# A hybrid Hyena/attention layer: output projection by Strassen's seven products instead of eight

## The chip, the cores and the metric

One NeuronCore of one Trainium2 chip. The metric is the device time of one execution in microseconds (us), lower is better. A measurement of this kernel tells differences of some 0.2% from none.

## The reference

One layer over 512 latent tokens and 256 context tokens of width 2048. The tokens are normalised and modulated, projected to 4928 columns, and go through three groups of heads (a long convolution, attention with 8 heads, and pooling), whose outputs side by side are again 2048 wide. The part that changes is the last product and what surrounds it:

```python
out_l = mixer(u_l, keys_all, lp, rope, True)      # (1, 512, 2048)
x_l = x_l + gt * (out_l @ w_out[l])               # w_out: (2048, 2048), gt: (1, 1, 2048)
return rmsnorm(x_l, final_norm_g)                 # over the 2048 columns of each token
```

## The kernel before

All five engines run programs of their own, written out by hand, and wait for each other on semaphores; the order of work on an engine is the order in the code. DMAs are issued by SyncE (SP), a few by ScalarE.

TensorE multiplies rounded float32 numbers only, so every operand x is split in two: ScalarE writes its rounded part (`_hi`), VectorE the remainder x - hi (`_lo`), and TensorE sums three products, hi*hi, hi*lo and lo*hi. The 2048 columns of the mixed heads lie transposed in the tile UG, 16 blocks of 128 rows with 512 tokens each: 0 to 3 from the convolution, 4 to 11 from attention, 12 to 15 from pooling.

The output projection goes by four blocks b of 512 output columns and four pieces c of 512 rows of w_out, 16 pieces of 1 MB. For each piece n = 4b + c:

- SyncE loads it to one of three places `wo_raw` once the piece three before it is done (`load_out`, L547).
- ScalarE rounds it into one of two tiles `wo_hi` once the piece two before it is done (`wo_high`, L1031); VectorE writes the remainder over the raw weights (`wo_low`, L1687).
- TensorE multiplies it by four groups of 128 tokens, each 4 x 3 products into its own PSUM bank (`out_part`, L2370), 48 products in all. The stationary operand is the left side (128 x 128), the moving one the weights (512 columns).

The left side is split once, by block of UG (`mixed`, L1021 and L1675). At the end of a block b VectorE multiplies each token group's bank by the gate (L1695) and adds x (L1697, tile `y`), ScalarE takes the squares (L1038), and GpSimd multiplies by the gain (L657). For the last block the gate is multiplied into the weights instead (`gate_into`, L1683), and the four token groups end one after another: sum, squares, root, reciprocal, scaling (L1697, L1038, L1197, L1922, L1203, L1926, L1927), then the stores.

The first piece's four groups are spread between the last steps of attention, as fillers.

## Time and profile before

| | |
|---|---|
| median of 3 runs | 921.84 us (921.84 to 921.89) |
| span of the profiled execution | 920.1 us, 1.7 below that median |
| own time of the profiled execution | not listed apart from the span |
| TensorE matmuls | 906.8 us busy, 99% of the span |
| VectorE, ScalarE, GpSimd busy | 70%, 43%, 13% |
| output projection after attention | 749.9 to 913.1 us |
| after the last product | 7.0 us |

A busy share is a mean over stages with different limits. The durations of matmuls overlap: the distance from one start to the next counts, not the 0.39 us of one. "Idle before" is how long an engine stood still ahead of an instruction, with what released it.

### The profile page before, as it was taken

Reading aid. Unit: us, or ns where it says so; the run is one execution under the profiler, and the core shown is the slowest. Engines: PE = TensorE matmul, PEld = TensorE weight load, DVE = VectorE, ACT = ScalarE, POOL = GpSimd, SP = SyncE. Lnnn points to the kernel's source line nnn. Section 1 sums busy time; section 2 is a strip of 40 time slices with the busy share of each in tenths; the row PEclk is TensorE's granted clock in tenths of the full one; section 3 lists DMA queues with packets and bytes.
Section 4 is the critical chain, followed back from the end, with each engine's and each line's share of the span. In section 5 each row is a group of like instructions: output and inputs, shape, how many; then the busy total and the mean of one; then the engine's idle time right before and its main releaser. Section 6 shows DMA issues by size and latency. Waiting matters only on the chain.

```text
span 920.1 us, 12214 instructions
## 1 busy us (share of the span) xinstructions
PE 906.8 (99%) x4850; PEld 756.7 (82%) x4850; DVE 641.1 (70%) x839; ACT 396.0 (43%) x615; POOL 115.6 (13%) x107
## 2 busy tenths in 40 slices
PE   9999999999999999999999999999999999999996
PEld 6777788888888888888888888889999888888885
DVE  5555898799987899867974674877777961424463
ACT  4655566535435344333233434554544551322124
POOL 1222200300003000001007731000010000202020
PEclk9999999999999999999999999999999999999999
DMA  9999923223322212287872352201010244233214
GB/s 361 416 420 422 413 101 104 92 80 97 109 82 91 69 69 92 70 323 285 298 275 93 92 172 70 69 30 40 1 58 1 92 188 179 92 101 114 105 46 182
DMA packets 29860, 137.93 MB, mean 150 GB/s; under 512 B 3531, under 2 KB 3915, under 8 KB 22892
## 3 DMA queue, kind: packets, MB, share of 16 engines
q1 hardware_dynamic: 29328, 136.50, 40.0%
q8 instruction: 38, 0.62, 0.3%
q10 hardware_dynamic: 476, 0.66, 0.2%
q14 instruction: 18, 0.15, 0.1%
HBM read 131.25 MB, written 4.19 MB: 147 GB/s over the span
## 4 chain that ended last, share of the span: by engine, by line
PE 89%; DMA 5%; DVE 2%; ACT 2%; issue 1%; SPq 0%; POOL 0%; ACTq 0%; DVEq 0%
PE pp L2058 40%; PE pp L2370 19%; PE pp L2088 17%; DMA ada_raw<-in_w_ada_dram 5%; PE pp L1973 3%; PE pp L1949 2%; PE pp L2334 2%; PE pp L1979 1%; PE pp L2326 1%; PE pp L2325 1%; DVE softmax_stats L1644 1%; ACT U L996 1%; DMA ada_raw<-in_w_scale_dram 1%; DVE pt_lo L1659 0%; PE pp L2157 0%
## 5 line engine op out<-in xcount | busy, mean ns | idle before, releaser
L2058 PE MATMUL pp<-h_hi,w_hi 128*128 128x512 f32 x544 | 213.0, 392 | 0.0
L2058 PE MATMUL pp<-h_hi,w_lo 128*128 128x512 f32 x544 | 211.8, 389 | 0.0
L2058 PE MATMUL pp<-h_lo,w_hi 128*128 128x512 f32 x544 | 211.8, 389 | 0.0
L1359 DVE TENSOR_TENSOR w_lo<-w_raw,w_hi 128x1024 fp32r<-128x1024 f32 x68 | 89.3, 1313 | 68.6 <-ACT w_hi L787 67.9
L787 ACT ACTIVATE w_hi<-w_raw 128x1024 fp32r<-128x1024 f32 x68 | 71.8, 1056 | 129.4 <-PE pp L2058 129.4
L2058 PEld LDWEIGHTS pp<-h_hi,w_lo 128*128 128x128 f32 x544 | 102.1, 188 | 21.5
L2058 PEld LDWEIGHTS pp<-h_hi,w_hi 128*128 128x128 f32 x544 | 102.2, 188 | 21.1 <-DVE w_lo L1359 0.3
L2058 PEld LDWEIGHTS pp<-h_lo,w_hi 128*128 128x128 f32 x544 | 102.2, 188 | 20.5
L2370 PE MATMUL pp<-wo_hi,m_hi 128*128 128x512 f32 x256 | 99.7, 390 | 0.0
L2370 PE MATMUL pp<-wo_hi,m_lo 128*128 128x512 f32 x256 | 99.6, 389 | 0.0
L2370 PE MATMUL pp<-wo_lo,m_hi 128*128 128x512 f32 x256 | 99.6, 389 | 0.0
L1687 DVE TENSOR_TENSOR wo_lo<-wo_raw,wo_hi 128x2048 fp32r<-128x2048 f32 x16 | 36.7, 2291 | 82.4 <-ACT wo_hi L1031 82.4
L1031 ACT ACTIVATE wo_hi<-wo_raw 128x2048 fp32r<-128x2048 f32 x16 | 30.6, 1914 | 86.9 <-PE pp L2370 86.9
L2370 PEld LDWEIGHTS pp<-wo_hi,m_lo 128*128 128x128 f32 x256 | 48.1, 188 | 10.1
L2370 PEld LDWEIGHTS pp<-wo_hi,m_hi 128*128 128x128 f32 x256 | 48.0, 188 | 10.0
L2370 PEld LDWEIGHTS pp<-wo_lo,m_hi 128*128 128x128 f32 x256 | 48.1, 188 | 9.8
L1004 ACT ACTIVATE pt_hi<-pp 128x768 fp32r<-128x768 f32 x32 | 26.0, 812 | 50.3 <-PE pp L2334 50.0
L1659 DVE TENSOR_TENSOR pt_lo<-pp,pt_hi 128x768 fp32r<-128x768 f32 x32 | 30.4, 952 | 19.1 <-ACT pt_hi L1004 19.1
L996 ACT ACTIVATE U<-pp,softmax_stats 128x768 f32<-128x768 f32 x32 | 28.9, 904 | 23.8 <-DVE softmax_stats L1646 23.6
L657 POOL TENSOR_TENSOR y<-y,gain 128x512 f32<-128x512 f32 x12 | 15.5, 1297 | 180.0 <-ACT out_tmp L1038 179.7
L1371 DVE SCALAR_TENSOR_TENSOR gate_acc<-w_gate_raw,silu_c,gate_acc 128x2048 f32<-128x2048 f32 x15 | 35.2, 2346 | 1.5 <-DMA w_gate_raw<-in_w_gate_dram 1.5
L1949 PE MATMUL pp<-ada_raw,silu_spread 128*32 128x256 f32 (+1 forms) x544 | 32.3, 378 | 3.9 <-DMA ada_raw<-in_w_ada_dram 2.7
(348 smaller groups left out, 1794.0 us busy)
## 6 DMA issues: line engine op xcount, KB each, us to landing
w_raw<-in_wb_dram SPq DMA_DIRECT2D x68, 512.0 KB, 3.7
ada_raw<-in_w_ada_dram SPq DMA_DIRECT2D x15, 2048.0 KB, 13.4
w_gate_raw<-in_w_gate_dram SPq DMA_DIRECT2D x16, 1024.0 KB, 6.4
wo_raw<-in_w_out_dram SPq DMA_DIRECT2D x16, 1024.0 KB, 4.7
y<-in_x_dram SPq DMA_DIRECT2D x4, 1024.0 KB, 8.5
wa_raw<-in_wa_dram SPq DMA_DIRECT2D x14, 288.0 KB, 8.0
UG<-in_xT_dram SPq DMA_DIRECT2D x7, 512.0 KB, 8.8
wh_raw<-in_w_heads_dram SPq DMA_DIRECT2D x4, 768.0 KB, 4.6
```

The lines of the kernel that those rows point to most:

```text
L787: eng.activation(lane(wb_hi, n % 2), lane(wb_raw, n % KW), ACT.Copy).then_inc(wb_hi_done, 1)
L996: eng.activation(prob(n % 3).rearrange("p (a b) -> p a b", a=2), psum[:, 2 * (n % 2):2 * (n % 2) + 2, 0:384], ACT.Exp, bias=st[:, 4 * s + ...
L1031: eng.activation(wo_high_[n % 2][:], wo_raw[n % 3][:], ACT.Copy).then_inc(wo_hi, 1)
L1359: eng.tensor_tensor(lane(wb_lo, n % KW), lane(wb_raw, n % KW), lane(wb_hi, n % 2), ALU.subtract).then_inc(wb_lo_done, 1)
L1371: eng.scalar_tensor_tensor(out=gate_acc[:], in0=w, scalar=c, in1=gate_acc[:], op0=ALU.mult, op1=ALU.add).then_inc(row_sums, 1)
L1659: eng.tensor_tensor(lo, psum[:, 4:6, :].rearrange("p a b -> p (a b)")[:, 0:LK].rearrange("p (k q) -> p k q", k=6), hi, ALU.subtract).then_ ...
L1687: eng.tensor_tensor(wo_low_[n % 3][:], wo_raw[n % 3][:], wo_high_[n % 2][:], ALU.subtract).then_inc(wo_lo, 1)
L1949: mm = eng.matmul(ps[7][32 * strip:32 * strip + 32, 256 - n:256], spread[:, 32 * kk:32 * kk + 32], ada[b % 3][:, kk * n:(kk + 1) * n], sta ...
L1973: mm = eng.matmul(ps[i][:], w, x, start=first and n == 0, stop=last and n == len(xs) - 1)
L2058: mm = eng.matmul(ps[i][:], w, x, start=(kk == 0 and m == 0), stop=(kk == KT - 1 and m == 2))
L2088: mm = eng.matmul(dst, w, x, start=first and m == 0, stop=last and m == 2)
L2370: mm = eng.matmul(psum[:, 4 * (b % 2) + tok, :], a, v[:, w:w + L], start=(kk == 0 and m == 0), stop=(kk == 15 and m == 2))
```

## The change

Tokens, rows and columns are each halved: the left side A into A11, A12, A21, A22 (tokens x rows of w_out; the row halves are pieces 0, 3 and 1, 2 of each column block, so the blocks of UG 0 to 3, 12 to 15 and 4 to 11), w_out into B11 to B22. Seven products of halves, numbered 1 to 7, take the place of eight; each is two column blocks b by two pieces c, 28 chunks in the order of `CHUNKS`, of 24 products each (two token groups). Their left sides are single halves or differences, their right sides single halves (products 1, 2, 3) or sums of halves of w_out.

- The sums of weights are made by DMA: SyncE loads one piece to a place `wo_sum` (`load_sum`), and GpSimd issues DMAs that add another piece of w_out to it in place (`add_weights`); the sums of 7, 6 and 4 are made one from the other.
- The left sides of 7, 6, 5 and 3 are made by GpSimd (`side`), in halves of 1024 columns, over UG itself but for that of 7. All left sides are split when their product comes (`side_high`, `side_low`), not once.
- Products 2, 4, 5 and 3 go on accumulating in the banks that hold 1, 7, 6 and 6 + 5 (`BANKS`); what other blocks need of products 1 and 7 is copied out by ScalarE (`hold`), 6 without 1 by VectorE (`without_first`), and GpSimd multiplies the copies by the gate and subtracts them from x ahead of time (`subtract_ahead`).
- The gate is multiplied on VectorE for all blocks (`block_out`). The tokens 256 to 511 end first (`LAST_TOKENS`), and the last two groups in one chunk, 27.
- x is loaded in two halves, y_left and y_right, the second after chunk 17, since it lies where the side of 6 was.

```diff
+CHUNKS = [(1, 0, 0), (1, 1, 0), (1, 0, 1), (1, 1, 1)] + [(u, b, c) for u, b in (
+    (7, 0), (6, 0), (4, 0), (2, 0), (2, 1), (7, 1), (6, 1), (4, 1), (5, 0), (5, 1), (3, 0), (3, 1)) for c in range(2)]
...
+SIDES = (1, 7, 6, 4, 2, 5, 3)
+PLACE = {1: 0, 7: 1, 6: 2, 4: 3, 2: 0, 5: 0, 3: 3}
...
+def summed(n):
+    u, b, c = CHUNKS[n]
+    if u == 5:
+        return (c + 2, 1, 1) if b == 0 else (c, 3, 7)
+    return c, b + 1, 3 * b + {7: 1, 6: 2, 4: 3}[u]
...
+            eng.wait_ge(wo_mm, chunk_of(7, 1, 1) + 1)
+            for c in range(2):
+                load_sum(chunk_of(5, 0, c))
+            eng.wait_ge(wo_mm, chunk_of(6, 1, 1) + 1)
+            for i in range(4):
+                eng.dma_start(y_right[:, 2 * i * L:2 * (i + 1) * L], t["x"][i * P:(i + 1) * P, 1024:D]).then_inc(y_in[1], 16)
+            for c in range(2):
+                eng.wait_ge(wo_lo, chunk_of(4, 1, c) + 1)
+                load_sum(chunk_of(5, 1, c))
+            for n in range(24, 28):
                 load_out(n)
...
+            def side(u, c):
+                if u == 7:
+                    made(eng.tensor_tensor(side_raw(7, c), mixed_part(0, 0, c), mixed_part(0, 1, c), ALU.subtract))
...
+            def add_weights(n):
+                u, b, c = CHUNKS[n]
+                i, loads, added = summed(n)
+                if u in (6, 4):
+                    eng.wait_ge(sum_added[i], 16 * added - 16)
+                    eng.wait_ge(wo_lo, chunk_of(7 if u == 6 else 6, b, c) + 1)
+                else:
+                    eng.wait_ge(sum_in[i], SUM_FROM[i] + 16 * loads)
+                eng.dma_start(wo_sum[i][:], w_out(u == 4, u in (7, 5), b, c), accum_op=ALU.add).then_inc(sum_added[i], 16)
...
+            def subtract_ahead(b):
+                g = gate_rows_[:, (2 + b) * L:(3 + b) * L]
+                eng.wait_ge(held6, 2 * b + 2)
+                for x in (product1[b], product7[b]):
+                    link(eng.tensor_tensor(x[0][:], x[0][:], g, ALU.mult))
+                    link(eng.tensor_tensor(x[1][:], x[1][:], g, ALU.mult))
+                for i in range(2):
+                    y = y_block(2 + i, 2 + b)
+                    link(eng.tensor_tensor(y, y, product7[b][i][:], ALU.subtract))
+                    eng.tensor_tensor(y, y, product1[b][i][:], ALU.subtract).then_inc(side_made, 1)
...
...
+            eng.wait_ge(y_in[1], 32 + 64)
+            eng.wait_ge(held, 8)
+            add_weights(chunk_of(5, 1, 0))
+            subtract_ahead(0)
+            add_weights(chunk_of(5, 1, 1))
+            subtract_ahead(1)
+            gains((2, 1), (3, 1), (2, 2), (3, 2), (2, 3), (3, 3), (0, 2), (1, 2))
...
+            side_high(1, 1)
             wo_high(2)
-            for k in range(8, 16):
-                mixed(k)
-            for n in range(3, 16):
+            wo_high(3)
+            side_high(7, 0)
+            hold(1, 0)
+            wo_high(4)
...
+                if n == 16:
+                    hold(7, 1)
+                    side_high(5, 1)
+                if n == 20:
+                    side_high(3, 0)
+                if n == 21:
+                    row_squares(2, 1)
+                    row_squares(3, 1)
...
+                if n == 25:
+                    for tok in range(2, 4):
+                        row_squares(tok, 3)
+                    for i in range(2):
+                        last_root(i)
+                        last_scale(i)
...
+            def block_out(tok, b):
+                half = b % 2
+                u = (3 if tok < 2 else 5) if b >= 2 else (2 if tok < 2 else 4)
+                n = chunk_of(u, half, 1)
+                eng.wait_ge(wo_mm, n + 1 + (n == 27 and tok == 1))
+                bank, g, y = ps[BANKS[u][half] + tok % 2][:], gate_rows_[:, b * L:(b + 1) * L], y_block(tok, b)
+                dst = bank
+                if u == 4:
+                    eng.wait_ge(held6, 2 * half + 2)
+                    link(eng.tensor_tensor(bank, bank, part6[tok % 2][:], ALU.subtract))
+                if b >= 2:
+                    eng.wait_ge(side_made, 8 + 4 * half + (tok - 1 if tok >= 2 else tok + 3))
+                if u == 5:
+                    dst = part6[tok % 2][:]
+                link(eng.tensor_tensor(dst, bank, g, ALU.mult))
+                eng.tensor_tensor(y, dst, y, ALU.add).then_inc(res_done, 1)
...
-            def gate_into(n):
-                eng.wait_ge(wo_in[n % 3], 16 * (n // 3) + 16)
-                w = wo_raw[n % 3].rearrange("p (k c) -> p k c", k=4)
-                g = gate_rows_[:, 3 * L:4 * L]
-                g = bass.AP(tensor=g.tensor, offset=g.offset, ap=[list(g.ap[0]), [0, 4], list(g.ap[1])])
-                eng.tensor_tensor(w, w, g, ALU.mult).then_inc(wo_gated, 1)
...
+            def out_part(n, tok):
+                u, b, c = CHUNKS[n]
                 eng.wait_ge(wo_lo, n + 1)
-                hi, lo = wo_high_[n % 2], wo_low_[n % 3]
+                eng.wait_ge(mix_lo, 2 * SIDES.index(u) + c + 1)
+                hi, lo, x_hi, x_lo = wo_high_[n % 2], wo_low_[n % 3], side_hi[PLACE[u]], side_lo[PLACE[u]]
                 for k in range(4):
-                    kk = 4 * c + k
...
```

**GpSimd, the last third of the output projection.** Before, the last rows of its order are the split of the pooling weights and then the gains, with no DMA:

```order
L644 TENSOR_TENSOR pool_lo0_163<-U,pool_hi0_159 128x512 [waits pool_step_p]
L647 CAST w_pool_hi_167<-w_pool_122 128x512 [waits wh_lo_done]
L648 TENSOR_TENSOR w_pool_lo_168<-w_pool_122,w_pool_hi_167 128x512 [waits pool_step_p]
L657 TENSOR_TENSOR y_152<-y_152,gain_151 128x512 [waits sq_done_o,x_rows_and_gain_in]
L657 TENSOR_TENSOR y_152<-y_152,gain_151 128x512 [waits sq_done_o] x11
```

Now accumulating DMAs (L770) stand in its order. The last two are those of chunk 22 (wo_sum0) and chunk 23 (wo_sum1); between them stands the first `subtract_ahead` (L783 to L791):

```order
L770 DMA wo_sum0_142<-in_w_out_dram 128x2048 [waits wb_in0,product_held,x_in1]
L783 TENSOR_TENSOR product1_00_149<-product1_00_149,gate_rows_146 128x512 [waits part6_held]
L784 TENSOR_TENSOR product1_01_150<-product1_01_150,gate_rows_146 128x512 [waits pool_step_p]
L783 TENSOR_TENSOR product7_00_153<-product7_00_153,gate_rows_146 128x512 [waits pool_step_p]
L784 TENSOR_TENSOR product7_01_154<-product7_01_154,gate_rows_146 128x512 [waits pool_step_p]
L787 TENSOR_TENSOR y_right_148<-y_right_148,product7_00_153 128x512 [waits pool_step_p]
L788 TENSOR_TENSOR y_right_148<-y_right_148,product1_00_149 128x512 [waits pool_step_p]
L787 TENSOR_TENSOR y_right_148<-y_right_148,product7_01_154 128x512
L788 TENSOR_TENSOR y_right_148<-y_right_148,product1_01_150 128x512 [waits pool_step_p]
L791 TENSOR_TENSOR y_right_148<-y_right_148,product1_00_149 128x512
L791 TENSOR_TENSOR y_right_148<-y_right_148,product1_01_150 128x512
L770 DMA wo_sum1_143<-in_w_out_dram 128x2048 [waits wb_in1]
```

The DMA for a chunk of weights now has ten GpSimd operations of other work in front of it.

**ScalarE, the splits of the weights near the end.** Before, four squares stand between the roundings of pieces 13 and 14:

```order
L1031 ACTIVATE wo_hi1_149<-wo_raw1_143 128x2048 [waits wo_gated,wo_bank_mm,wo_in1]
L1038 ACTIVATE out_tmp_153,row_sums_154<-y_152 128x512 [waits sq_done_o,y_done_o] x4
L1031 ACTIVATE wo_hi0_148<-wo_raw2_144 128x2048 [waits wo_gated,wo_mm,wo_in2]
L1031 ACTIVATE wo_hi1_149<-wo_raw0_142 128x2048 [waits wo_gated,wo_mm,wo_in0]
L1038 ACTIVATE out_tmp_153,row_sums_154<-y_152 128x512 [waits sq_done_o,y_done_o]
```

Now, from the rounding of chunk 19 to the rounded half side ahead of chunk 22:

```order
L1214 ACTIVATE wo_hi1_141<-wo_sum1_143 128x2048 [waits wo_mm,weight_sum1_added]
L1214 ACTIVATE wo_hi0_140<-wo_sum2_144 128x2048 [waits wo_mm,weight_sum2_added]
L1200 ACTIVATE side_hi3_128<-UG 128x1024 [waits wo_mm,side_made]
L1214 ACTIVATE wo_hi1_141<-wo_sum3_145 128x2048 [waits wo_mm,weight_sum3_added]
L1226 ACTIVATE out_tmp_159,row_sums_160<-y_left_147 128x512 [waits sq_done_o,y_done_o] x2
L1200 ACTIVATE side_hi3_128<-UG 128x1024 [waits wo_mm,side_made]
L1214 ACTIVATE wo_hi0_140<-wo_sum0_142 128x2048 [waits wo_mm,weight_sum0_added]
```

The weights' rounding comes twice as often, and half sides and squares that wait for VectorE stand ahead of the next one. The scalings of the token groups (L1197, L1203) stood behind the last rounding, that of piece 15:

```order
L1031 ACTIVATE wo_hi0_148<-wo_raw2_144 128x2048 [waits wo_gated,wo_mm,wo_in2]
L1031 ACTIVATE wo_hi1_149<-wo_raw0_142 128x2048 [waits wo_gated,wo_mm,wo_in0]
L1038 ACTIVATE out_tmp_153,row_sums_154<-y_152 128x512 [waits sq_done_o,y_done_o]
L1197 ACT_TABLE_LOAD [waits row_sum]
L1197 ACTIVATE row_scale_155<-row_sums_154,row_scale_155 128x1 [waits sq_done_o]
L1203 ACTIVATE y_152<-y_152,row_scale_155 128x512 [waits gained,row_scale_done]
L1203 ACTIVATE y_152<-y_152,row_scale_155 128x512
```

Now the scalings of two groups (L1232, L1240) stand between the roundings of chunks 25 (wo_raw1) and 26 (wo_raw2):

```order
L1226 ACTIVATE out_tmp_159,row_sums_160<-y_right_148 128x512 [waits sq_done_o,y_done_o] x2
L1214 ACTIVATE wo_hi0_140<-wo_raw0_134 128x2048 [waits wo_mm,ada_in0]
L1214 ACTIVATE wo_hi1_141<-wo_raw1_135 128x2048 [waits wo_mm,ada_in1]
L1226 ACTIVATE out_tmp_159,row_sums_160<-y_right_148 128x512 [waits sq_done_o,y_done_o] x2
L1232 ACT_TABLE_LOAD [waits row_sum]
L1232 ACTIVATE row_scale_161<-row_sums_160,row_scale_161 128x1 [waits sq_done_o]
L1240 ACTIVATE y_left_147<-y_left_147,row_scale_161 128x512 [waits gained,row_scale_done]
L1240 ACTIVATE y_left_147<-y_left_147,row_scale_161 128x512
L1232 ACTIVATE row_scale_161<-row_sums_160,row_scale_161 128x1 [waits row_sum,sq_done_o]
L1240 ACTIVATE y_left_147<-y_left_147,row_scale_161 128x512 [waits gained,row_scale_done]
L1240 ACTIVATE y_left_147<-y_left_147,row_scale_161 128x512
L1214 ACTIVATE wo_hi0_140<-wo_raw2_136 128x2048 [waits wo_mm,ada_in2]
```

What was the very end of the order before is now, for two of the four token groups, ahead of two roundings.

## Rows read from the trace of the kernel before

**Rows 1.** The page: busy time and share; clock in 40 slices.
```profile
PE 906.8 (99%) x4850; PEld 756.7 (82%) x4850; DVE 641.1 (70%) x839; ACT 396.0 (43%) x615; POOL 115.6 (13%) x107
...
PEclk9999999999999999999999999999999999999999
```

**Rows 2.** The chain that ended last, in order of time: start, length, work.
```profile
749.87 163.21 PE pp L2370 x720
```

**Rows 3.** Windows: length; busy of PE, PEld, DVE, ACT, POOL; clock; DMA share; GB/s.
```profile
750.00:913.10 163.10, 163.07 (x720) 134.69 (x718) 69.26 (x72) 45.61 (x61) 15.53 (x12) 1.00 0.34 126
913.10:920.10 7.00, 0.00 (x0) 0.00 (x0) 2.00 (x4) 2.35 (x5) 0.00 (x0) 0.69 0.57 217
```

**Rows 4.** The tile wo_raw (ns min/median/max), then one piece on two engines.
```profile
L547 SPq DMA_DIRECT2D wo_raw<-in_w_out_dram x16: 328/328/334, 685.2 to 880.5; - x16
L1683 DVE TENSOR_TENSOR wo_raw<-wo_raw,gate_rows x4: 2282/2292/2293, 852.6 to 886.7; 128x2048 f32<-128x2048 f32 x4
...
760.84 1.92 ACT L1031 ACTIVATE wo_hi<-wo_raw 128x2048 fp32r<-128x2048 f32 x1 [7.09 <-PE pp L2370]
762.79 2.29 DVE L1687 TENSOR_TENSOR wo_lo<-wo_raw,wo_hi 128x2048 fp32r<-128x2048 f32 x1 [4.78 <-ACT wo_hi L1031]
```

**Rows 5.** Timeline, idle time between the last heads (idle before, releaser).
```profile
738.98 0.81 ACT L1004 ACTIVATE pt_hi<-pp 128x768 fp32r<-128x768 f32 x1 [4.58 <-PE pp L2334]
739.67 0.75 DVE L1670 SCALAR_TENSOR_TENSOR UG<-pp,first_in,UG 128x512 f32<-128x512 f32 x1 [3.33 <-PE pp L2088]
```

**Rows 6.** Copies of ScalarE: one PSUM bank (timeline), 1024 columns (page).
```profile
715.55 0.60 ACT L976 ACTIVATE v_hi<-pp 128x512 fp32r<-128x512 f32 x1
...
L787 ACT ACTIVATE w_hi<-w_raw 128x1024 fp32r<-128x1024 f32 x68 | 71.8, 1056 | 129.4 <-PE pp L2058 129.4
```

**Rows 7.** Timeline of VectorE: gate and sum of a token's block.
```profile
786.76 0.69 DVE L1695 TENSOR_TENSOR pp<-pp,gate_rows 128x512 f32<-128x512 f32 x1
787.49 0.69 DVE L1697 TENSOR_TENSOR y<-pp,y 128x512 f32<-128x512 f32 x1
788.10 0.69 DVE L1695 TENSOR_TENSOR pp<-pp,gate_rows 128x512 f32<-128x512 f32 x1
```

**Rows 8.** Timeline of the end: last token, and ScalarE's table load before.
```profile
900.97 1.28 ACT L1197 ACT_TABLE_LOAD   x1
902.27 0.29 ACT L1197 ACTIVATE row_scale<-row_sums,row_scale 128x1 f32<-128x1 f32 x1
...
913.10 0.69 DVE L1697 TENSOR_TENSOR y<-pp,y 128x512 f32<-128x512 f32 x1 [2.28 <-PE pp L2370]
915.11 0.48 DVE L1926 TENSOR_SCALAR y<-y,row_scale 128x512 f32<-128x512 f32 x1
915.51 0.74 DVE L1927 SCALAR_TENSOR_TENSOR y<-y,row_scale,gain 128x512 f32<-128x512 f32 x1
...
915.11 1.33 ACT L1203 ACTIVATE y<-y,row_scale 128x512 f32<-128x512 f32 x2 [0.23 <-DVE row_scale L1922]
```

**Rows 9.** Window while x is loaded; median time to landing (page).
```profile
755.00:765.00 10.00, 10.00 (x46) 8.29 (x45) 5.22 (x7) 1.92 (x1) 0.00 (x0) 1.00 1.01 419
...
wo_raw<-in_w_out_dram SPq DMA_DIRECT2D x16, 1024.0 KB, 4.7
```

**Rows 10.** The tile y, GpSimd's multiply: ns min/median/max.
```profile
L657 POOL TENSOR_TENSOR y<-y,gain x12: 1292/1296/1302, 789.1 to 882.7; 128x512 f32<-128x512 f32 x12
```

**Rows 11.** VectorE's remainder of 1024 columns, then both engines from 546 us.
```profile
L1359 DVE TENSOR_TENSOR w_lo<-w_raw,w_hi x68: 1207/1226/2879, 123.1 to 546.6; 128x1024 fp32r<-128x1024 f32 x68
...
546.26 1.30 POOL L644 TENSOR_TENSOR pool_lo<-U,pool_hi 128x512 fp32r<-128x512 f32 x1
547.50 1.61 POOL L643 CAST pool_hi<-U 128x512 fp32r<-128x512 f32 x1
549.20 2.68 POOL L644 TENSOR_TENSOR pool_lo<-U,pool_hi 128x512 fp32r<-128x512 f32 x1
...
546.63 2.01 DVE L1359 TENSOR_TENSOR w_lo<-w_raw,w_hi 128x1024 fp32r<-128x1024 f32 x1 [1.95 <-ACT w_hi L787]
```

507 lines of the change are left out of this document (346 added, 161 removed).

## The prediction

> **What bounds the kernel now.** I read the page first, then the chain of waits, then the stretch of the output projection by itself. The page shows TensorE busy 99% of the span at full clock in every slice [rows 1]; the chain of waits says that nothing else decides: its longest piece is 720 products of the output projection in 163.21 us without a gap, 0.2267 us each [rows 2]. In that stretch VectorE is busy 42% of the time, ScalarE 28%, GpSimd 10%, and the DMA engines 34% [rows 3]. So fewer products shorten the kernel one for one, as long as the other engines keep each piece of weights ready. That is what I check.
>
> **How much time a piece leaves.** ScalarE starts the rounded part of a piece when the piece two before it is done; VectorE's remainder starts 1.95 us later and takes 2.29 [rows 4]: 4.24 us, with the semaphores 4.3. Before, a piece kept TensorE for 48 x 0.2267 = 10.88 us. Now it has half the rows of the left side, 24 products, 5.44 us, and the same 4.3 us of splitting: the slack falls from 6.6 us to 1.1. Whatever ScalarE or VectorE does ahead of a split beyond 1.1 us is a stall of TensorE.
>
> **The change, term by term** (T is the end of a chunk, numbers as in CHUNKS; S is the start).
>
> Removed: 8 products of 96 become 7, 768 - 672 = 96 products: 96 x 0.2267 = **-21.8**. The fillers between the last heads stay 48 products; ScalarE and VectorE have 4.58 and 3.33 us of idle time there [rows 5], which takes the second split that moves forward; 0. Also gone are four multiplies of weights by the gate on VectorE, 2.29 each [rows 4], which hid beside TensorE; 0.
>
> Waits that the written order makes, with every sum in time: **+9.7**.
> Chunk 4 (T the end of chunk 2): ScalarE takes product 1 out of the banks first (two copies of 0.6 [rows 6]), rounds the weights (1.9), then the second half of side 7 (1.06, from the 1024-column row [rows 6]); VectorE's order has both halves of that side (1.2) ahead of the weights' remainder (2.2). T + 1.2 + 1.9 + 1.1 + 1.2 + 2.3 = T + 7.7 where 5.4 is wanted: +2.3.
> Chunk 17: two copies and a half side (2.2) stand ahead of its rounding, 2.2 + 4.3 = 6.5: +1.1.
> Chunk 22 (T the end of chunk 19): VectorE's block (2,1) is three linked operations, 0.73 + 0.73 + 0.61 = 2.07 [rows 7], then half a side 1.2 (VectorE's 1024 columns [rows 11]), remainder 21 (2.2) to T + 5.5, block (3,1) to 7.5; ScalarE squares it (0.8), rounds a half side (1.0) to 9.4, and only then rounds piece 22, ready at 9.4 + 4.2 = 13.6 where 10.9 is wanted: +2.7.
> Chunk 26 (T the end of chunk 23): blocks (2,3), (3,3) and remainder 25 end at T + 4.9, the mean 0.3, table load and root 1.6, then the reciprocal and two scalings, 1.5 [rows 8], T + 8.3; the second token's chain another 1.9; then 4.2 for the piece: 14.4 against 10.9, +3.6.
>
> Tail: the last token came 5.44 us after the one before; now 2.72. VectorE is held by the token before for 0.73 (its gate, no longer folded into the weights) + 3.15 (from its sum to the end of its scalings [rows 8]) = 3.9 us, 1.2 beyond the last product, then a gate of its own, 0.73: **+1.9**.
>
> The accumulating DMAs: 16 of 1 MB, issued by GpSimd; the trace has none. From below, each is a plain load: 2.5 us of the engines at 419 GB/s, 4.7 us from issue to landing [rows 9]. From above, it loads, reads the sum back and writes: three passes, 7.5 us of engines, 9.7 to landing. I take two passes, one read more than the load (5.0 and 7.2), the middle. For the issue on GpSimd I take 0.8 us, between SyncE's 0.33 [rows 4] and GpSimd's own 1.3 for 512 columns. The Trainium skill's page Collectives: The Full Stack, section "The bandwidth ceiling", says that a reducing copy reads two sources on one ring and moves at half the rate of a plain one; no run here shows it yet, and by it the sum would be the two-pass one.
> *Chains.* In 7, 6, 4 each sum is made from the one before, so a step is 0.8 + 7.2 + 4.2 = 12.2 us against two chunks, 10.9: +1.3, twice, less the slack of 1.1, on two halves: **+3**. By one pass nothing.
> *Traffic.* From S8 to S12 (21.8 us) there are two sums, three loads, the gain (1 MB) and the accumulates of 9, 14, 15; from S16 to S20 the accumulates 18 to 21, two sums and 2 MB of x. By two passes both are about 12.6 MB, 30 us at 419 GB/s: +8 each, **+16**. By one pass about 9 MB: within 1 us of the time.
> *Chunk 23.* Its accumulate stands in GpSimd's order behind the first subtract_ahead, which needs y_right, which is loaded only after chunk 17 (T). x and one sum, 3.1 MB, 7.5 + 2.6 us: T + 10; accumulate 22, 0.8; ten GpSimd operations of 1.3, most linked (0.09): 13.8, T + 24.7; then 0.8 + 7.2 + 4.2 = T + 36.9, where 27.2 + 2.7 (chunk 22's wait) is due: **+7**. By one pass +4.5. Part of the wait of 16 to 20 falls inside this time and is not paid twice: **-8**.
>
> GpSimd beside VectorE. GpSimd's multiply is 1.30 us in every one of 12 rows, each taken when VectorE reads PSUM and one tile [rows 10]. But a remainder of VectorE (two inputs in SBUF) that began 0.37 us into a GpSimd operation took 2.01 us in place of 1.23, and one took 2.88; two GpSimd operations beside it and the next took 1.61 and 2.68, the first of them a copy [rows 11]. One waits for the other's whole operation. New work of GpSimd: 8 sums of sides at about 2.5 (1024 columns, twice 512), 20 subtractions and multiplies, 14 gains, some 66 us; VectorE's splits with two SBUF inputs: 73 us. So three remainders (6.6) and a half side (1.2) fall into the first subtract_ahead: +7.8 at 23; two into the second and the gains that chunk 26's scalings wait for: +4.4; a side's sum at chunk 3: +1. **+13**. By no exclusion 0. The Trainium skill's page SBUF — State Buffer, "Who interferes with whom", states that rule for a VectorE instruction with two SBUF inputs beside a GpSimd one that reads SBUF; the rows agree.
>
> Sum: -21.8 + 9.7 + 1.9 + 3 + 16 + 7 - 8 + 13 = +20.8. The profiled execution's span is 920.1 us, and the runs' median, 921.84, lies 1.7 us above it; what lies outside the span is not touched. 921.84 + 20.8 = 942.6, **942**.
>
> **Rivals.**
> One pass (an accumulate costs what a load does): -21.8 + 9.7 + 1.9 + 0 + 1 + 4.5 + 13 = +8.3, **930**. For it: the engines are busy only 34% now. Chance 0.22.
> Faster: the sums are never late. If they are there when ScalarE asks, at 6 to 9, 14 to 23, only order and tail are left: -21.8 + 9.7 + 1.9 = -10.2, **912**. It needs accumulates that land within 6 us and a subtract_ahead that is through 7 us sooner than I work out; it decides as soon as all lateness beyond the order's own is below 8.4 us. Against it: the 13.8 us of GpSimd work ahead of accumulate 23 come from twelve rows that agree. Chance 0.22.
> Three passes: each traffic stretch grows to 16.8 MB, 40 us, +18 in place of +8, and each chain step by 2.5: about +28, **970**. Chance 0.12.
> The forecast itself 0.42; and 0.02 for a result that is no change by accident. The products surely fall to 672, so "no effect of the change" is no rival. The clock stays out of the sum: it was 1.00 under products and 0.69 in the 7 us after the last one [rows 3], so a stall of 8 us may leave the next products slower, at most a chunk's 5.4 us more each; that is inside the upper bound.
>
> **How the numbers follow.** The two-pass case alone gives 932 to 954. The range takes in one pass and most of the faster case, and stops short of the whole of the three-pass one: 913 to 966, with 1 in 10 outside on each side. What a measurement of this kernel can tell from no change is 0.2%, 1.8 us. Faster is the rival of that name, 0.22; of the one-pass case a little lies at 920 to 924, same 0.04; the rest, 0.74, is slower.
>
> **What would show it.** Products: 672, 0.227 us each where they run. Idle time of TensorE in front of chunks 4, 17, 22 and 26 of 2.3, 1.1, 2.7 and 3.6 us, released by VectorE's remainder: the order. Idle in front of 6 to 9 and 10 to 12, 18, 19, with ScalarE waiting for the DMA of a weight sum: passes and traffic; the time to landing (4.7, 7.2 or 9.7) tells which. Chunk 23 as the longest single wait, 7 us or more, behind the first subtractions. VectorE's remainders of 2.3 us that read 2.5 to 3.6 beside GpSimd. The prediction is wrong if accumulates land as loads do, if GpSimd's subtractions are through in under 10 us, or if an accumulate's issue holds GpSimd for several us each, which would be late everywhere.

## The result: 970.6 us, 5.3% slower, where 942 was forecast

The changed kernel takes 970.58 us (median of 4 runs, 968.97 to 971.44), the kernel before 921.87 beside it: ratio 1.0526, 95% interval 1.0511 to 1.0541. The sign was forecast, the size was not: +48.7 us against +20.8, outside the range of 913 to 966. One of the eleven executions of e9_short_fill below, the profiled one, took 1272 us at a mean granted clock of 0.66 and is left out of that kernel's figures.

The page of the changed kernel (profiled execution: span 968.6 us) answers to [rows 1]: busy time of the engines, TensorE and its clock in 40 slices, and the queue of the accumulating DMAs.

```profile
PE 902.9 (93%) x4754; PEld 746.6 (77%) x4754; DVE 683.6 (71%) x857; ACT 426.7 (44%) x633; POOL 191.6 (20%) x153
...
PE   9999999999999999999999999999999896968475
...
PEclk9999999999999999999999999999999898998888
...
q0 software_dynamic: 2304, 16.78, 9.0%
```

TensorE has 96 products fewer (4850 to 4754), but holes in nearly every slice after the 31st, and in six of these nine slices its mean granted clock is below 0.9 of full speed (digit 8). Queue q0 moves the 16 accumulated pieces of 1 MB: 9.0% of 968.6 us, 87.2 us of all 16 engines, 5.45 each.

The chain that ended last (start, length, work), pieces of it between 742 and 931 us. A DMA of wo_sum is a plain load (869.90) or an accumulate (the others shown); L2671 are the products of the output projection.

```profile
742.48 15.18 DMA wo_raw<-in_w_out_dram
...
761.97 7.89 PE pp L2671 x24
...
775.65 7.96 DMA wo_sum<-in_w_out_dram
...
788.42 8.03 DMA wo_sum<-in_w_out_dram
...
801.11 13.15 DMA wo_raw<-in_w_out_dram
...
818.58 8.50 PE pp L2671 x24
...
839.40 8.13 DMA wo_sum<-in_w_out_dram
...
852.34 13.28 DMA wo_sum<-in_w_out_dram
...
869.90 18.09 DMA wo_sum<-in_w_out_dram
...
888.56 0.86 POOL wo_sum L770
...
909.30 9.40 DMA wo_sum<-in_w_out_dram
918.73 1.92 ACT wo_hi L1214
920.67 2.30 DVE wo_lo L1921
...
923.02 7.60 PE pp L2671 x24
```

In [rows 2] this stretch was one piece of 720 products. Now the chain goes from DMA to DMA and touches TensorE only between them. An accumulate that meets nothing else takes 8.0 us from its issue to ScalarE's rounding (775.65, 788.42, 839.40); the forecast had 0.8 + 7.2. In the stretches in which the DMA engines are full the same 1 MB takes 13 to 18 us in this chain, plain or accumulating. From 888.56 to 909.30 stands the first subtract_ahead, 20 us.

Two windows, with the columns of [rows 3]: chunks 5 and 6 with the end of 4 and the wait ahead of 7, then chunk 18:

```profile
770.00:788.00 18.00, 16.55 (x73) 12.96 (x71) 10.41 (x7) 11.47 (x11) 1.72 (x2) 1.00 0.91 172
...
870.00:878.30 8.30, 8.30 (x24) 6.33 (x24) 1.07 (x2) 0.72 (x1) 0.00 (x0) 0.65 1.03 252
```

In the first the DMA engines are busy 0.91 of the time, where the whole stretch had 0.34 before. In the second, after 6.3 us without products, the mean granted clock was 0.65: the products began at the lower level (1.2 GHz, 0.43 us apart) and ended at the upper (2.4 GHz, 0.227). That chunk took 8.25 us in place of 5.44.

The table adds up the places from TensorE's timeline: idle time ahead of the chunks plus what their 24 products took beyond 5.44 us, in us. (Idle time runs here from 0.227 us after the start of the last product; the figure in the profile's rows is 0.16 us smaller where there is a wait.) The forecast's +13 for GpSimd beside VectorE lies in it as 1 at chunk 3, 7.8 at 23 and 4.4 at 26, which makes +21.0 of its rounded +20.8. The last column is e8_small_short, an experiment below in which both sums cost next to nothing.

| place | forecast | changed kernel | e8_small_short |
|---|---|---|---|
| last heads | 0 | 1.8 | 1.5 |
| chunks 3, 4 | 3.3 | 7.1 | 2.3 |
| 6 to 9 | 3 | 3.9 | 0.2 |
| 10 to 12 | 8 | 11.7 | 2.4 |
| 16, 17 | 1.1 | 1.8 | 1.1 |
| 18, 19 | 8 | 14.7 | 1.5 |
| 20 to 22 | 2.7 | 5.1 | 5.3 |
| 23 | 14.8 | 14.5 | 0 |
| overlap | -8 | - | - |
| 24 to 27 | 8.0 | 7.4 | 5.8 |
| others | 0 | 0.3 | 0.2 |
| tail | 1.9 | 2.0 | 2.0 |
| products removed | -21.8 | -21.8 | -21.8 |
| sum | +21.0 | +48.5 | +0.5 |

The spans differ by 48.5 and 0.3 us, so nothing large is missing from the table. Of the 66.5 us in the third column from chunks 3, 4 to "others", 13.5 are slow products in chunks 3, 11, 18, 19, 23 and 26. What each row is worth when it is taken away is another question, and the experiments answer it differently than the table suggests.

### The profile page after: what moved, and what is told of

Its sections match the earlier page's. It is cut to its first block, busy times and chain, and to the rows that moved or that the text cites. A ratio compares the mean times of both kernels' runs of the same rounds, so it can differ in the third digit from the quotient of the medians.

```text
span 968.6 us, 12203 instructions
## 1 busy us (share of the span) xinstructions
PE 902.9 (93%) x4754; PEld 746.6 (77%) x4754; DVE 683.6 (71%) x857; ACT 426.7 (44%) x633; POOL 191.6 (20%) x153
## 4 chain that ended last, share of the span: by engine, by line
PE 72%; DMA 13%; DVE 6%; ACT 4%; POOL 2%; issue 2%; SPq 0%; ACTq 0%; POOLq 0%; DVEq 0%
PE pp L2361 38%; PE pp L2391 15%; DMA wo_sum<-in_w_out_dram 7%; PE pp L2671 5%; PE pp L2276 4%; DMA ada_raw<-in_w_ada_dram 3%; DMA wo_raw<-in_w_out_dram 3%; DVE wo_lo L1921 2%; PE pp L2252 2%; ACT wo_hi L1214 2%; PE pp L2637 2%; PE pp L2282 1%; PE pp L2629 1%; PE pp L2628 1%; DVE softmax_stats L1882 1%
## 5 line engine op out<-in xcount | busy, mean ns | idle before, releaser
L2671 PE MATMUL pp<-wo_hi,side_hi 128*128 128x512 f32 x224 | 94.9, 424 | 48.9 <-DVE wo_lo L1921 33.0
L2671 PEld LDWEIGHTS pp<-wo_hi,side_hi 128*128 128x128 f32 x224 | 45.1, 202 | 65.3 <-DVE wo_lo L1921 37.4
L2671 PE MATMUL pp<-wo_lo,side_hi 128*128 128x512 f32 x224 | 92.1, 411 | 0.0
L2671 PE MATMUL pp<-wo_hi,side_lo 128*128 128x512 f32 x224 | 92.0, 411 | 0.0
L1921 DVE TENSOR_TENSOR wo_lo<-wo_sum,wo_hi 128x2048 fp32r<-128x2048 f32 x16 | 38.1, 2384 | 52.7 <-ACT wo_hi L1214 52.7
L1214 ACT ACTIVATE wo_hi<-wo_sum 128x2048 fp32r<-128x2048 f32 x16 | 30.5, 1912 | 56.9 <-DMA wo_sum<-in_w_out_dram 50.8
L2671 PEld LDWEIGHTS pp<-wo_hi,side_lo 128*128 128x128 f32 x224 | 45.1, 201 | 10.3
L2671 PEld LDWEIGHTS pp<-wo_lo,side_hi 128*128 128x128 f32 x224 | 45.3, 202 | 9.3
L1921 DVE TENSOR_TENSOR wo_lo<-wo_raw,wo_hi 128x2048 fp32r<-128x2048 f32 x12 | 30.1, 2507 | 24.1 <-ACT wo_hi L1214 24.1
L1166 ACT ACTIVATE U<-pp,softmax_stats 128x768 f32<-128x768 f32 x32 | 28.9, 903 | 23.8 <-DVE softmax_stats L1884 23.7
L704 POOL CAST sum_hi<-U 128x768 fp32r<-128x768 f32 (+1 forms) x2 | 2.5, 1234 | 185.4 <-DVE U L1770 119.9
```

The costliest lines, as they stand in the source:

```text
L1166: eng.activation(prob(n % 3).rearrange("p (a b) -> p a b", a=2), psum[:, 2 * (n % 2):2 * (n % 2) + 2, 0:384], ACT.Exp, bias=st[:, 4 * s + ...
L1214: eng.activation(wo_high_[n % 2][:], src[:], ACT.Copy).then_inc(wo_hi, 1)
L1921: eng.tensor_tensor(wo_low_[n % 3][:], src[:], wo_high_[n % 2][:], ALU.subtract).then_inc(wo_lo, 1)
L2671: mm = eng.matmul(ps[BANKS[u][b] + tok][:], a, v[:, w:w + L], start=u in (1, 7, 6) and c == 0 and k == 0 and m == 0, stop=c == 1 and k == ...
```

## The experiments

All ratios are to the kernel before, with 95% intervals. The kernels of e3, e6, e7, e10, e11 and e12 compute everything; the others leave out part of the sums or add filler products, so only their times count. Code lines are excerpts.

### e1_plain: plain loads for the accumulates

```diff
-eng.dma_start(wo_sum[i][:], w_out(u == 4, u in (7, 5), b, c), accum_op=ALU.add).then_inc(sum_added[i], 16)
+eng.dma_start(wo_sum[i][:], w_out(u == 4, u in (7, 5), b, c)).then_inc(sum_added[i], 16)
```

> The 16 accumulating DMAs become plain loads of the same 1 MB from GpSimd's queue, so that the sum of the two pieces is left out: the output is not the reference's. Theory (an accumulate costs the DMA engines two passes): undisturbed, issue to ScalarE's rounding took 8.0 us for pieces 6, 7, 16, 17 and should fall to about 5.5; the idle time of TensorE ahead of chunks 7 to 9 (3.3 us) goes, ahead of 11 and 12 (8.6) and of 18 and 19 (10.2) falls to 1 or 2 each, ahead of 3 (4.9) to 2, ahead of 23 (12.6) to about 8.6, and with the long stalls goes most of the time that slow products take after them (13.5 to about 5): 968.6 - 26 - 8.5, about 934 us. Rival (the pass is cheap; the order of the queues and GpSimd's issues make the lateness): landing stays near 8 us and the time above 960.

946.8 us, 1.0265 (1.0248 to 1.0283): 23.8 less than the changed kernel, between theory and rival. From its page, the queue:

```profile
q0 software_dynamic: 2304, 16.78, 4.8%
```

4.8% of its span of 946.0 us is 45.4 us, 2.84 for each 1 MB, where the accumulate took 5.45. So an accumulate costs the engines 1.9 times a load. The forecast took two passes, 5.0. By the Trainium skill, page Collectives: The Full Stack, section "The bandwidth ceiling", the reducing step of a collective moves at half the rate of a copy; 5.45 against 2.84 agrees. Where nothing else was on the engines, the plain loads landed 5.1 us after their issue, in place of 8.0. The waits ahead of 7 to 9 went, that of 18 fell to 3.5 and that of 19 to nothing, that of 23 to 5.1. The time did not reach 934: slow products fell only from 13.5 to 11.9 us, where the theory had 5, chunk 11 still waited 3.9 us and the wait of 26 rose to 5.4.

### e2_small: accumulates of 64 KB

```diff
-eng.dma_start(wo_sum[i][:], w_out(u == 4, u in (7, 5), b, c), accum_op=ALU.add).then_inc(sum_added[i], 16)
+eng.dma_start(wo_sum[i][:, 0:128], w_out(u == 4, u in (7, 5), b, c)[:, 0:128], accum_op=ALU.add).then_inc(sum_added[i], 16)
```

> Each of the 16 accumulating DMAs covers 128 of 2048 columns (64 KB in place of 1 MB), so that most of the sum is left out: the output is not the reference's. With plain loads in their place the kernel took 946.8 us, 22 to 24 less. Theory (most of the lateness is bytes on the DMA engines): without these 16 MB the stalls ahead of chunks 3, 11 and 18 (2.9, 3.9 and 3.5 us with plain loads) fall to about 1 each, that of chunk 23 (5.1) stays, since GpSimd's 20 us of subtractions ahead of its accumulate stay: about 938. Rival (what matters is that another DMA stands in each chain, whatever its size): 944 or more.

937.8 us, 1.0174 (1.0157 to 1.0191). The theory held in its number: with the issues and waits all in place, it is the bytes. Nearly all of them together are worth 32.8 us: 23.8 for the second pass, 9.0 for the first. The waits ahead of 3, 11 and 18 fell to 0, 0.4 and 1.2 us. Not foreseen was that the wait ahead of 26 rose from 3.7 to 7.8 us: the first scalings, which stand ahead of remainder 26 on VectorE, waited 4.1 us for GpSimd's gains (L776).

### e3_ahead23: accumulate 23 ahead of the subtractions

```diff
-            subtract_ahead(0)
             add_weights(chunk_of(5, 1, 1))
+            subtract_ahead(0)
             subtract_ahead(1)
```

> The accumulate of piece 23 is issued ahead of the first subtract_ahead on GpSimd instead of behind it; nothing is left out. Theory (chunk 23 is late because its accumulate stands behind 20.2 us of GpSimd work): it is issued at about 890 us, lands by 899, is wanted at 910: the 12.6 us idle ahead of chunk 23 fall to 1 or less, its 24 products run in 5.4 us, not 7.4: 13 to 14 us less, about 955. Rival (its DMA would be late anyway, behind the loads of x and of the two last sums): the wait stays above 8 us and the time above 963.

969.0 us, 1.0511 (1.0496 to 1.0527): nothing gained beyond the spread of the runs. The theory was right on the wait and wrong on the time, the rival right on the time and wrong on the wait. TensorE's timeline shows the first product of chunks 23, 25 and 26 (start, length; idle before it and its releaser at the end):

```profile
912.22 0.50 PE L2671 MATMUL pp<-wo_hi,side_hi 128*128 128x512 f32 x1 [0.54 <-DVE wo_lo L1921]
...
930.12 0.79 PE L2671 MATMUL pp<-wo_hi,side_hi 128*128 128x512 f32 x1 [6.69 <-DVE wo_lo L1921]
...
944.80 0.77 PE L2671 MATMUL pp<-wo_hi,side_hi 128*128 128x512 f32 x1 [6.33 <-issue]
```

The 12.4 us ahead of 23 are 0.5, as the theory said. But 6.7 us now stand ahead of 25 (1.6 before) and 6.3 ahead of 26 (3.7), and three chunks run slow. VectorE's blocks of the right half wait for the subtractions, and its remainders stand behind the blocks:

```profile
922.19 0.69 DVE L1946 TENSOR_TENSOR part<-pp,gate_rows 128x512 f32<-128x512 f32 x1 [5.36 <-POOL y_right L788]
```

So the place of that accumulate alone was not the bound. GpSimd's two subtract_ahead, 38 us of work together, stand behind it, and whoever needs them first shows the wait; e4_short_sub tests that.

### e4_short_sub: the same, and the subtractions on 8 columns

```diff
-g = gate_rows_[:, (2 + b) * L:(3 + b) * L]
+g = gate_rows_[:, (2 + b) * L:(2 + b) * L + 8]
...
-link(eng.tensor_tensor(x[0][:], x[0][:], g, ALU.mult))
+link(eng.tensor_tensor(x[0][:, 0:8], x[0][:, 0:8], g, ALU.mult))
```

> As e3_ahead23, and each of the 20 GpSimd operations of subtract_ahead works on 8 of 512 columns: most of the subtraction of products 1 and 7 is left out, the output is not the reference's. In e3_ahead23 the 12.6 us ahead of chunk 23 went, and 6.9 and 6.5 us came ahead of chunks 25 and 26 in their place, and the time stayed at 969. Theory (the 40 us of GpSimd's two subtract_ahead are the chain there, whichever chunk waits for them, and GpSimd's operations lengthen VectorE's remainders): the waits ahead of 25 and 26 fall to the order's own, 1.6 and 3.7, remainder 21 takes 2.3 us in place of 3.4, chunks 22, 25 and 26 run fewer slow products: 13 to 16 us less, about 954. Rival (other work fills the place once more, the accumulates or VectorE's blocks): above 963.

953.9 us, 1.0338 (1.0320 to 1.0356), as the theory said: against e3_ahead23, which has the same order, GpSimd's 20 operations are worth 15.1 us; with the order it is 16.7 against the changed kernel. The waits ahead of 25 and 26 became 0 and 3.9 us. Its timeline also shows most clearly that GpSimd and VectorE exclude each other (the lock, from here on), GpSimd first, then VectorE:

```profile
892.09 2.13 POOL L784 TENSOR_TENSOR product<-product,gate_rows 128x8 f32<-128x8 f32 x1
894.30 0.20 POOL L783 TENSOR_TENSOR product<-product,gate_rows 128x8 f32<-128x8 f32 x1
...
891.87 2.29 DVE L1921 TENSOR_TENSOR wo_lo<-wo_sum,wo_hi 128x2048 fp32r<-128x2048 f32 x1
```

An operation of 8 columns, 0.20 us by itself, took 2.13 and ended with VectorE's remainder.

### e5_fill: products in the stalls, to hold the clock

```diff
+FILL = {3: 20, 11: 28, 18: 28, 19: 15, 23: 52, 26: 15}
...
+for m in range(count):
+    eng.matmul(ps[BANKS[u][b]][:], x[:, (m % 8) * P:(m % 8 + 1) * P], x[:, 0:L], start=False, stop=False, skip_group_check=True)
 eng.wait_ge(wo_lo, n + 1)
```

> Filler products on TensorE ahead of the waits of chunks 3, 11, 18, 19, 23 and 26 (20, 28, 28, 15, 52, 15 of 0.227 us, each total shorter than the idle time there); they add to a bank of the chunk, so the output is not the reference's. No wait is moved. Theory (after a stall of 3.5 us or more the granted clock is at its lower level, and the products run 0.427 us apart in place of 0.227, whatever else goes on): these six chunks run in 5.4 to 5.6 us in place of 7.2 to 8.3, 13.5 us less in all, about 955. Rival (those products are slow because weights are read beside full DMA engines, which is so at 11, 18 and 19): the lengths stay and the time stays at 966 to 969.

969.7 us, 1.0520 (1.0503 to 1.0537): nothing gained. The window of chunk 18, to be read beside the one of the changed kernel above:

```profile
872.50:878.00 5.50, 5.50 (x26) 4.55 (x25) 0.91 (x2) 0.00 (x0) 0.00 (x0) 1.00 1.02 250
```

The clock is 1.00 beside equally full DMA engines (1.02), so the rival's reason, contention, is out: five of the six chunks ran in 5.44 to 5.60 us, only 19 in 7.2 (its fillers ended 3.0 us before its wait did), 11.1 us less in the six. Yet the time stayed. Chunk 6 waited 2.6 us where it had waited for nothing, 12 waited 4.1 where it had 1.7, and these and 21 now ran slow, 6.1 us more together; the other 5 us came back as idle time. A chunk that ends sooner only waits longer for the next piece, as long as the pieces come from a chain of DMAs and GpSimd.

### e6_late_left: the left half of x behind piece 3

```diff
 eng.wait_ge(pv_mm, 8)
+eng.wait_ge(wo_hi, 4)
 for i in range(4):
     eng.dma_start(y_left...
```

> The load of the left half of x (2 MB, 4 DMAs) waits until the rounding of piece 3 has begun; nothing is left out. Theory (piece 3 lands late, at 757.7 us, because its 1 MB shares full engines with two accumulates and with this x): chunk 3's idle time falls from 4.7 to about 2 us, its slow products (7.7 us long) to about 6, and chunk 4 shows about 1 us of the order's own wait: 3 us less, 965 to 966. Rival (the accumulates of 4 and 5 alone fill the engines): no change, 968 to 969.

971.8 us, 1.0534 (1.0508 to 1.0560): nothing gained, as the rival said. Chunk 3 waited 3.4 us in place of 4.7, but it waited 3.2 us in the profiled executions of e4_short_sub and e7_order26 too, where nothing ahead of it was changed, so this difference can't be put down to the edit. At chunk 11 there were 7.3 us of idle time in place of 6.5.

### e7_order26: piece 26 ahead of the roots

```diff
+                    wo_high(26)
                     for i in range(2):
                         last_root(i)
                         last_scale(i)
```

(and the remainder on VectorE alike.)

> The rounding and the remainder of piece 26 are moved ahead of the roots and scalings of the first two tokens on ScalarE and VectorE; nothing is left out. Theory (the 3.7 us idle ahead of chunk 26 are this order's, and only the tail lies behind them, so that nothing can take their place): the wait falls below 1 us, the products of 26 run in 5.5 us in place of 7.2: 5 us less, 964 to 965. Rival (GpSimd's gains or the load of piece 26 hold it): 968 or more.

965.7 us, 1.0475 (1.0458 to 1.0493): 4.8 us gained, as the theory said. In the profiled execution chunk 26 lost its wait and its slow products, 5.5 us, and 1.8 us of wait came back ahead of chunk 27. (The spans differ by 2 us more; that lies ahead of chunk 26, where the two kernels are the same.) Behind the last chunk only the tail is left, +2.0 us in both, and it took nothing of the gain back.

### e8_small_short: both sums next to free

The edits of e2_small and e4_short_sub together.

> The small accumulates of e2_small and the short subtractions and the order of e4_short_sub together; both sums are mostly left out, the output is not the reference's. Theory (removed products -21.8, the written order's waits +9.7, the tail +1.9, and everything else was the two sums): 912, with some slow products after the one wait of 3.6 us 914, so faster than before. Rival (the loads that remain are late by themselves at half the time for each piece): 922 or more.

923.1 us, 1.0017 (1.0006 to 1.0028): the rival's number. The two edits nearly add up: 970.6 - 923.1 = 47.5 us, singly 32.8 and 16.7. And what is left is no gain: the 21.8 us of removed products are spent entirely. The timeline's first products of chunks 22 and 26, and a window over the second:

```profile
871.22 0.47 PE L2671 MATMUL pp<-wo_hi,side_hi 128*128 128x512 f32 x1 [2.91 <-issue]
...
898.80 0.47 PE L2671 MATMUL pp<-wo_hi,side_hi 128*128 128x512 f32 x1 [3.92 <-issue]
```

```profile
899.00:906.00 7.00, 7.00 (x25) 5.54 (x25) 5.67 (x9) 1.45 (x4) 4.52 (x2) 0.76 0.01 2
```

The waits of the written order were there (1.9 us at 4, 0.3 at 17, 3.1 at 22, 4.1 at 26, against 2.3, 1.1, 2.7 and 3.6), but also 1.4 at 12, 1.3 at 18 and 0.6 and 0.5 at 10 and 16, which the forecast had not listed, and two slow chunks of 1.7 us each. The rival's reason, late loads, fits only 10 and 18, where ScalarE's rounding waited for a DMA: 1.9 us. Ahead of 12 it stood behind a square that waited for VectorE's block, so again the written order, and ahead of 16 the remainder took 3.7 us in place of 2.3 beside GpSimd's gains.

### e9_short_fill: the same, with fillers ahead of 22 and 26

```diff
+FILL = {22: 10, 26: 14}
```

> e8_small_short with filler products on TensorE ahead of the waits of chunks 22 and 26 (10 and 14 of 0.227 us, each total shorter than the idle time there, 3.1 and 4.1 us); most of both sums is left out and the fillers add to a bank: the output is not the reference's. In e8_small_short these two chunks ran 7.18 us each in place of 5.44 at the lower clock. Theory (where the chain that ends last runs over TensorE's products, slow ones cost their whole length, though in e5_fill, where it ran over DMAs and GpSimd, they cost nothing): both run in 5.5 us, 3.4 less than the 923.1, about 919.7. Rival (VectorE and ScalarE bind there too, and idle time takes their place): 922.5 or more.

920.8 us, 0.9992 (0.9983 to 1.0001): 2.3 us less than e8_small_short, two thirds of the 3.4. No trace shows where the rest went. Where TensorE's products are the chain, as here, the lower clock does cost time.

### e10_dma_order: wanted first, issued first

```diff
 load_out(2)
-load_sum(5)
 load_out(3)
+load_sum(5)
...
+eng.wait_ge(wo_hi, chunk_of(2, 0, 1) + 1)
 for c in range(2):
     add_weights(chunk_of(7, 1, c))
...
 add_weights(chunk_of(4, 1, 0))
-add_weights(chunk_of(5, 0, 0))
 add_weights(chunk_of(4, 1, 1))
+add_weights(chunk_of(5, 0, 0))
```

(and on SyncE the loads in that order, the gain and both halves of x behind them.)

> Only the order of the DMAs is changed, nothing is left out: what is wanted first is issued first. Piece 3 ahead of the sum of 5, the left half of x behind piece 3; pieces 10 and 11 ahead of the sums and accumulates of 14 and 15, the gain behind pieces 12 and 13; the sum of 21 behind the landing of accumulate 18, accumulate 19 ahead of 20, the right half of x last. Theory (the stalls are bytes in the wrong order, the stretches as a whole have room): ahead of 3 and 11 the idle time falls from 4.9 and 6.7 us to 1 or 2, of 18 and 19 from 10.2 to about 6, with slow products gone 15 us less in all, about 954. Rival (the bytes of the accumulates fill the engines in any order, or chunk 23's chain over GpSimd takes the gain up): 964 or more.

961.1 us, 1.0426 (1.0410 to 1.0441): 9.4 us gained, between theory (954) and rival (964). Chunks 3 and 11 wait for nothing, 18 and 19 for 2.2 and 0.1. But 4.3 us came ahead of chunk 4, 2.5 ahead of 13 and 6.9 ahead of 21, and the 12 us ahead of 23 stood.

### e11_pool_order: GpSimd's order alone

```diff
+            multiply_ahead(0)
             for c in range(2):
                 add_weights(chunk_of(7, 1, c))
...
-            eng.wait_ge(y_in[1], 32 + 64)
             eng.wait_ge(held, 8)
+            multiply_ahead(1)
             add_weights(chunk_of(5, 1, 0))
-            subtract_ahead(0)
             add_weights(chunk_of(5, 1, 1))
+            eng.wait_ge(y_in[1], 32 + 64)
+            subtract_ahead(0)
             subtract_ahead(1)
```

> Only GpSimd's order is changed, nothing is left out: of each subtract_ahead the four multiplies go where GpSimd waited (10.4 us ahead of accumulate 14, 24.3 us ahead of accumulate 22), and both last accumulates go ahead of the subtractions. Theory (GpSimd's 40 us of subtract_ahead were the chain from 888 us on; eight of its 20 operations then fit into idle time): chunk 23's 12.6 us go, and 25 and 26 do not take them up as in e3_ahead23, about 956, near e4_short_sub's 953.9. Rival (the twelve operations left still hold VectorE's blocks and its remainders beside them): 963 or more.

963.1 us, 1.0440 (1.0419 to 1.0460): 7.5 us gained, just on the rival's side of its bound, though not for the rival's reason: chunk 23 waits 1.0 us, and 25 and 26 don't take it up. The moved multiplies have a price further up. They run beside the remainder of 10 and push the sums of sides beside that of 11; these took 3.4 and 5.3 us in place of 2.3, and the wait that was ahead of 11 stands ahead of 12 (6.7 us). The runs spread from 958.8 to 964.1, and the profiled one was the shortest.

### e12_all: the three orders together

> The orders of e10_dma_order, e11_pool_order and e7_order26 together, nothing left out. Theory (three separate places on the chain): 968.6 less 15, 13 and 5, about 937; still above the kernel before, since e8_small_short, with hardly any of the sums' work, took 923. Rival (they lie in the same chain, and one hides the other's gain): 950 or more.

948.6 us, 1.0291 (1.0277 to 1.0305): the sum of the single gains (9.4 + 7.5 + 4.8 = 21.7) is the 22.0 that came, though the first two were smaller than expected: by theory 937, by the rival 950 or more. None of the three orders takes another's gain, which speaks against the rival's reason. Two pieces of its chain, then a window around the first (columns as in [rows 3]) and the accumulates' queue in it (packets, MB, share of 16 engines):

```profile
866.69 22.91 DMA y_right<-in_x_dram
...
889.68 1.30 POOL y_right L793
```

```profile
852.00:889.00 37.00, 27.25 (x105) 21.29 (x103) 17.03 (x14) 11.10 (x11) 11.64 (x9) 0.86 1.03 283
```

```profile
q0 software_dynamic: 714, 5.19, 67.9%
```

For 37 us the DMA engines are full (1.03), two thirds of it with accumulates. An order within this stretch can't shorten it; whether some of its bytes could go earlier or later was not tried.

### e13_heads and e14_heads_26: what the written order leaves

e13 is e8_small_short with GpSimd's first sums held back until VectorE's last softmax scaling; e14 adds the order of e7_order26.

```diff
 eng.wait_ge(v_mm, 12)
+eng.wait_ge(p_done, 32)
 side(7, 0)
 side(5, 0)
```

> e8_small_short (both sums mostly left out), and GpSimd's first three sums of sides wait until VectorE's last softmax scaling is done. In the changed kernel a scaling of VectorE at 719.42 us, one input in SBUF, took 2.33 us in place of 0.62 beside a GpSimd sum from 718.94 to 721.34, and the last heads ended 1.8 us later than before. Theory (the wait for GpSimd's operation is these 1.8 us): the scaling takes 0.62, the first chunk after the heads starts 1.7 us sooner: 923.1 - 1.7, about 921.4. Rival (the side's remainder that VectorE has between the heads makes it): no change, 922.5 or more.

> e13_heads with the order of e7_order26 too: the best that the written order gives when the two sums cost hardly anything (they are mostly left out). Theory: in e8_small_short chunk 26 waited 4.1 us and ran 1.7 us longer; with these and the 1.7 us of the heads gone 923.1 - 7.5, about 916, 0.6% faster than before: what is left of the 21.8 us is eaten by the short pieces' own waits. Rival (the waits move to 27, as 1.9 us did in e7_order26): 918 to 920.

924.2 us, 1.0026 (1.0016 to 1.0036), and 923.3, 1.0016 (1.0007 to 1.0024): no gain from either; e13 came out on its rival's side, e14 above both of its forecasts. The mechanism of the heads is right. In the changed kernel, GpSimd's sum and VectorE's scaling:

```profile
718.94 2.40 POOL L751 TENSOR_TENSOR UG<-UG 128x1024 f32<-128x1024 f32 x1
...
719.42 2.33 DVE L1891 TENSOR_SCALAR U<-U,softmax_stats 128x768 f32<-128x768 f32 x1
```

In e13_heads the same scaling, then the remainder of piece 2 and the product that waited for it:

```profile
718.92 0.62 DVE L1892 TENSOR_SCALAR U<-U,softmax_stats 128x768 f32<-128x768 f32 x1
...
747.13 4.02 DVE L1922 TENSOR_TENSOR wo_lo<-wo_raw,wo_hi 128x2048 fp32r<-128x2048 f32 x1 [0.39 <-ACT wo_hi L1215]
...
751.21 0.50 PE L2672 MATMUL pp<-wo_hi,side_hi 128*128 128x512 f32 x1 [0.88 <-DVE wo_lo L1922]
```

The heads ran 1.2 us sooner, and then the postponed sums met remainder 2, which took 4.0 us in place of 2.3: the same wait in another place. (In e8_small_short that remainder took 2.3 us.) In e14_heads_26 the 3.9 us ahead of 26 moved to 27 (3.2 us, and that chunk ran 8.5 us).

## Why the forecast was wrong, step by step

**Right.** TensorE's products fell to 672. The waits of the written order at 4, 17, 22 and 26 were there, 9.3 us in e8_small_short for the 9.7 forecast (17 had 0.8 less and 26 0.5 more, so the sum agrees better than its parts). The tail was +2.0 for +1.9. The issue on GpSimd took 0.87 us for 0.8, an undisturbed accumulate 8.0 us to ScalarE for 0.8 + 7.2, and the engines 5.45 us for 5.0 (5.45 against 2.84 with plain loads). The chains of 6 to 9 cost 3.3 us of idle time for 3. Chunk 23 was the longest wait, 14.5 us with its slow products for 7 + 7.8. VectorE's remainders read up to 3.4 us beside GpSimd, as here in the changed kernel, the remainder of 21 and a multiply of subtract_ahead:

```profile
893.12 3.37 DVE L1921 TENSOR_TENSOR wo_lo<-wo_sum,wo_hi 128x2048 fp32r<-128x2048 f32 x1
...
894.42 3.22 POOL L784 TENSOR_TENSOR product<-product,gate_rows 128x512 f32<-128x512 f32 x1
```

**The step that failed first: the overlap of -8.** Traffic, chains, chunk 23 and the lock together were forecast at 3 + 16 + 7 - 8 + 13 = +31 and measured as 47.5 (970.6 - 923.1). The forecast let the wait of chunk 23 fall in part inside that of 18 to 20. It does not, since the chain of 23 is delayed by the same full engines. The forecast had x and the sum of 22 landed 10 us after the end of chunk 17, at the rate of free engines, although its own traffic term had them full at that time. Chunk 17 ended at 863.5; x landed at 885.5. The sum of 22 is loaded only when remainder 18 is done, at 869.90, and only when it has landed, at 888.0, does GpSimd go on to accumulates and subtractions: 25 us after chunk 17 in place of 10. These 15 us are as long as what chunks 18 and 19 lost, so nothing of 23's wait is hidden in theirs. Both stood at full length, 14.7 and 14.5 us. e3_ahead23 shows that the wait at 23 was no matter of one accumulate's place either.

**The traffic term was too small, and one stretch was not looked at.** 18 and 19 took 14.7 us for 8, and 10 to 12 took 11.7 for 8. Part of this is slow products (4.6 of the 14.7), but with fillers, in e5_fill, 18 and 19 still cost 14.7 us, 13.0 of them idle: the length is that of the DMA chain. From 742 us, where two loads of pieces, two accumulates, a sum and x compete, the forecast had no term; piece 3 took 15.2 us to land and chunks 3 and 4 cost 7.1 us for 3.3. The error of the method: it charged a stretch for bytes over rate less time, as if the piece wanted first landed first. e10_dma_order shows the difference: the same bytes in the order of need, 9.4 us less. All the accumulates' bytes together are worth 32.8 us by e2_small. Row by row the table's third column lies above the forecast by 8 us (the overlap), 6.7 (18, 19), 3.8 (3, 4), 3.7 (10 to 12), 2.4 (20 to 22) and 1.8 (heads), 26.4 of the 27.5 in all.

**The base was too good: -10.2 forecast, +1.2 measured.** That is removed products, order and tail, which e8_small_short leaves alone (923.1 against 921.9). Its table column shows 10.2 of these 11.4 us: 3.8 us of waits at 10, 12, 16 and 18; 3.5 us of slow products at 22 and 26, from the clock, which "stays out of the sum"; 1.5 in the last heads, costed at 0; and 0.1 to 0.2 us in each of eleven other chunks, 1.4 us in all. So the rival "faster", 912, was out of reach: with both sums nearly free the kernel is where it was. The slack of 1.1 us for each piece was worked out rightly and then used only at four places.

**The clock: left out for a poor reason, with less harm than the table suggests.** The six slow chunks take 13.5 us in the changed kernel. e5_fill took 11.1 us of them away and won nothing, since the chain ran over DMAs and GpSimd; in e9_short_fill, where it ran over TensorE, fillers won 2.3 of 3.4.

**GpSimd beside VectorE, +13.** As a term of its own it can't be told from the 20 us that subtract_ahead takes, itself 6 us longer than 13.8 because six of its ten operations stood beside VectorE's (894.42 above took 3.22 us for 1.30); e4_short_sub took both away for 16.7 us, where 7 + 7.8 + 4.4 had been forecast less the overlap. That GpSimd waits for VectorE's whole operation is shown by the row of 8 columns and 2.13 us, that VectorE waits for GpSimd's by the softmax scaling of 2.33 us.

**The rival of three passes,** "about +28, 970" (28 beyond the forecast), came closest in time for the wrong reason: an accumulate costs 1.9 passes. (Its first stretch was also counted too high: 15 transfers are 15.7 MB, not 16.8.)

What stays open: why e11_pool_order gained 7.5 us in its median and 11.6 in its profiled run, and where a third of the clock's cost went in e9_short_fill. No version ran faster than the kernel before beyond the noise, not even e9_short_fill with 0.9992: the best that computes everything is e12_all, 26.8 us slower, and its accumulates alone fill two thirds of the engines' time between 852 and 889 us.
